# Small products of h (routing logits, selection weights, forget gate) in four groups of 32 array columns

## What is computed

```python
# routing, first block
logit_g = (xt @ w_group + b_group)            # 4 columns
logit_e = (xt @ w_router + b_router)          # 16 columns
# even layer of the second block: weights of the 4 indexer heads that choose 128 keys a row
qa, ka, va, qi, ki, wi, qb, kb, vb = _split(xn @ w_in, EVEN_SPLITS)   # wi: 4 columns
score = jnp.einsum('bqhs,bqh->bqs', rel, wib)
# odd layer: forget gate of 8 heads
log_f = jax.nn.log_sigmoid(fc + forget_b)     # fc: 8 columns of xn @ w_in
f_cum = lax.cumsum(log_f, axis=1)             # added to the logits of the attention
```

## Time and profile before

| | |
|---|---|
| median of 3 runs | 1798.04 us (1797.51 to 1798.15) |
| the profiled execution's own time | 1798.52 us |
| its span (first to last instruction of the trace) | 1796.6 us |
| PE busy | 1772.3 us, 99% of the span |
| PEld, DVE, ACT, POOL busy | 1429.6, 1074.1, 932.5, 606.2 us |
| mean granted clock of PE | 0.996 of full speed |

### The profile page before, as it was taken

How to read it: one execution, slowest core, us unless ns; L and a number is a source line. 1 busy time by engine, 2 the same in 40 slices (tenths; PEclk the granted TensorE clock), 3 DMA queues, 4 the chain that set the end, 5 groups by cost and what they waited for, 6 DMA issues and landing times.

```text
span 1796.6 us, 24203 instructions
## 1 busy us (share of the span) xinstructions
PE 1772.3 (99%) x8498; PEld 1429.6 (80%) x8498; DVE 1074.1 (60%) x1971; ACT 932.5 (52%) x1601; POOL 606.2 (34%) x341
## 2 busy tenths in 40 slices
PE   7999999999999999999999999999999999999997
PEld 5888767888888777787888888887777888888887
DVE  6677747999999599855555554223345655555113
ACT  6667645888887355555444443223555544444221
POOL 2332233111111233233444444443431444444442
PEclk9999999999999999999999999999999999999999
DMA  8322246999997222332223323333431233223332
GB/s 307 136 72 83 81 166 215 365 382 389 382 385 304 68 82 85 92 94 71 94 94 100 100 94 97 97 100 106 139 97 36 94 103 97 94 95 100 98 97 69
DMA packets 71256, 258.78 MB, mean 144 GB/s; under 512 B 13547, under 2 KB 18795, under 8 KB 58744
## 3 DMA queue, kind: packets, MB, share of 16 engines
q1 hardware_dynamic: 66520, 250.19, 40.9%
q0 software_dynamic: 4640, 7.32, 1.1%
HBM read 247.52 MB, written 18.43 MB: 148 GB/s over the span
## 4 chain that ended last, share of the span: by engine, by line
PE 60%; DVE 5%; issue 0%; POOL 0%; DMA 0%; SPq 0%; ACT 0%; DVEq 0%
PE ps L215 18%; PE ps L216 18%; PE ps L217 18%; DVE selb L1369 2%; DVE m L1368 1%; PE ps L569 1%; PE ps L608 1%; PE ps L597 1%; DVE prob L798 1%; DVE prob L813 1%; PE ps L583 0%; PE ps L616 0%; DVE selb L1346 0%; PE ps L631 0%; PE ps L637 0%
## 5 line engine op out<-in xcount | busy, mean ns | idle before, releaser
L282 POOL TENSOR_TENSOR ring_wl<-ring_w,ring_wh 128x1024 fp32r<-128x1024 f32 (+1 forms) x224 | 528.6, 2362 | 904.2 <-ACT ring_wh L274 798.5
L215 PE MATMUL ps<-two_x_high,ring_wh 128*128 128x512 f32 x1064 | 418.8, 394 | 0.7 <-DVE nmax L798 0.6
L216 PE MATMUL ps<-two_x_low,ring_wh 128*128 128x512 f32 x1064 | 414.2, 389 | 0.0
L217 PE MATMUL ps<-two_x_high,ring_wl 128*128 128x512 f32 x1064 | 414.2, 389 | 0.0
L274 ACT CAST ring_wh<-ring_w 128x1024 fp32r<-128x1024 f32 (+1 forms) x228 | 235.8, 1035 | 224.8 <-PE ps L217 222.3
L215 PEld LDWEIGHTS ps<-two_x_high,ring_wh 128*128 128x128 f32 x1064 | 199.7, 188 | 46.9 <-issue 2.2
L216 PEld LDWEIGHTS ps<-two_x_low,ring_wh 128*128 128x128 f32 x1064 | 199.7, 188 | 42.0 <-issue 1.4
L217 PEld LDWEIGHTS ps<-two_x_high,ring_wl 128*128 128x128 f32 x1064 | 199.7, 188 | 41.7
L1125 ACT ACTIVATE acc<-ps,param 128x512 f32<-128x512 f32 x88 | 68.6, 780 | 172.0 <-DVE ps L1145 172.0
L215 PE MATMUL ps<-hid_high,ring_wh 128*128 128x512 f32 (+1 forms) x374 | 141.0, 377 | 0.0
L216 PE MATMUL ps<-hid_low,ring_wh 128*128 128x512 f32 (+1 forms) x374 | 140.8, 377 | 0.0
(11 more groups left out here) (366 smaller groups left out, 3256.0 us busy)
## 6 DMA issues: line engine op xcount, KB each, us to landing
ring_w<-in_w_ff_up SPq DMA_DIRECT2D x88, 512.0 KB, 3.6
one_wg<-in_w_gate SPq DMA_DIRECT2D x32, 1024.0 KB
one_wu<-in_w_up SPq DMA_DIRECT2D x32, 1024.0 KB
one_wd<-in_w_down SPq DMA_DIRECT2D x32, 1024.0 KB, 9.6
ring_w<-in_w_ff_down SPq DMA_DIRECT2D x32, 448.0 KB, 3.3
ring_w<-in_w_da SPq DMA_DIRECT2D x23, 512.0 KB, 3.9
ring_w<-in_w_ff_down SPq DMA_DIRECT2D x16, 512.0 KB, 3.5
ring_w<-in_w_rel SPq DMA_DIRECT2D x12, 512.0 KB, 3.7
```

The costliest lines, as they stand in the source:

```text
L215: mm(out, wh, xh, start=start, stop=False)
L216: mm(out, wh, xl, start=False, stop=False)
L217: return mm(out, wl, xh, start=False, stop=stop)
L282: eng.tensor_tensor(self.low[s][:, 0:k, :], self.slab[s][:, 0:k, :], self.high[s][:, 0:k, :].bitcast(F32), ALU.subtract).then_inc(self.spl ...
```

## The change

All three small projections become full fp32 products of weights and unsplit state. For the gate and the selection, POOL first multiplies the weights by the gain of the norm, so that the state is `h` itself; the rounding by ACT and the low parts are gone. Chunk j goes to the group of 32 array columns with the number j modulo 4, that is to PSUM partitions 32(j mod 4) and on; chunks 0 to 3 begin the four sums, 4 to 7 end them. The four partial sums are added by DVE: for the gate with a copy and three additions, for the other two in a reduction over four elements after the transposes, which are now of all 128 rows.

The order changes too. The logits of chunks 0 to 3 run in one go behind m = 5, 4 and 5 behind m = 7, 6 and 7 behind the transposes of chunk 6. Of the gate's products, four run before the first projection of the odd attention, and four, with the mean, inside it before its chunk 4. At the start of stage "two" ACT rounds two slabs before it computes the root, and DVE, not POOL, makes the rest of the first.

```diff
@@ Select
     def tensor_weigh(self, pe):
-        c, x, buf = self.c, self.norms.x, self.buf
+        c, buf = self.c, self.buf
         pe.wait_ge(self.w_ok, 1)
+        pe.wait_ge(self.norms.added, DC)
         for j in range(DC):
-            mm = c.product(c.ps[0:4, 3, :], (buf["wwh"][:, j, :], buf["wwl"][:, j, :]),
-                           (x[0][:, j, :], x[1][:, j, :]), j == 0, j == DC - 1)
-        mm.then_inc(self.weighed, 1)
+            at = 32 * (j % 4)
+            c.nc.tensor.matmul(c.ps[at:at + 4, 3, :], buf["ww"][:, j, :], c.h[:, j, :], start=(j < 4), stop=(j >= 4))\
+             .then_inc(self.weighed, 1)
...
         for tt in range(TT):
-            mm = nc.tensor.transpose(c.ps[:, 3, 8 * tt:8 * tt + 4], self.buf["wiT"][0:4, P * tt:P * tt + P],
-                                     c.k("ident")[0:4, 0:4])
+            mm = nc.tensor.transpose(c.ps[:, 3, P * tt:P * tt + P], self.buf["wiT"][:, P * tt:P * tt + P], c.k("ident"))
...
-        nc.vector.tensor_copy(wi[:, :, :], c.ps[:, 3, 0:8 * TT].rearrange("p (t e) -> p t e", t=TT)[:, :, 0:4])\
-          .then_inc(self.wi_ok, 1)
+        nc.vector.tensor_reduce(wi[:, :, :], c.bank(3).rearrange("p (t g e) -> p t e g", t=TT, g=4)[:, :, 0:4, :],
+                                AX_X, ALU.add).then_inc(self.wi_ok, 1)
@@ Gate
-    def tensor(self, pe, k):
-        c, buf, x = self.c, self.buf, self.norms.x
+    def tensor(self, pe, k, chunks):
+        c = self.c
         pe.wait_ge(self.w_ok, 1)
-        for j in range(DC):
-            pe.wait_ge(self.norms.xlow, 8 * k + j + 1)
-            mm = c.product(c.ps[0:8, 2, :], (buf["wfh"][:, j, :], buf["wfl"][:, j, :]),
-                           (x[0][:, j, :], x[1][:, j, :]), j == 0, j == DC - 1)
-        mm.then_inc(self.projected, 1)
+        for j in chunks:
+            at = 32 * (j % 4)
+            pe.wait_ge(self.norms.added, 8 * k + j + 1)
+            c.nc.tensor.matmul(c.ps[at:at + 8, 2, :], self.buf["wf"][:, j, :], c.h[:, j, :], start=(j < 4), stop=(j >= 4))\
+             .then_inc(self.projected, 1)
...
-        dve.wait_ge(self.projected, 1)
+        dve.wait_ge(self.projected, DC)
+        nc.vector.tensor_copy(x[:, :], c.ps[0:8, 2, :]).then_inc(self.joined, 1)
+        for group in range(1, 4):
+            dve.wait_ge(self.joined, group)
+            nc.vector.tensor_tensor(x[:, :], c.ps[32 * group:32 * group + 8, 2, :], x[:, :], ALU.add).then_inc(self.joined, 1)
+        dve.wait_ge(self.joined, 4)
         dve.wait_ge(self.norms.inverted, k + 1)
-        nc.vector.tensor_tensor(x[:, :], c.ps[0:8, 2, :], self.norms.rs[0:8, :], ALU.mult).then_inc(self.step, 1)
+        nc.vector.tensor_tensor(x[:, :], x[:, :], self.norms.rs[0:8, :], ALU.mult).then_inc(self.step, 1)
@@ Outward
+        def logits(chunks):
+            for i in chunks:
+                pe.wait_ge(self.whole_ok, i + 1)
+                group = slice(32 * (i % 4), 32 * (i % 4) + 32)
+                nc.tensor.matmul(c.ps[group, 2, :], wr[:, i, :], xw[:, i, :], start=(i < 4), stop=(i >= 4))\
+                  .then_inc(self.logits, 1)
...
-            if m == 3:
-                chunk(0)
-            chunk(m - 2)
-        chunk(6)
-        chunk(7, rows=False)
+            for i in (0, 1) if m == 3 else (m - 2,):
+                pe.wait_ge(self.whole_ok, i + 1)
+                if m == 7:
+                    logits((4, 5))
+                turn(i)
+            if m == 5:
+                logits(range(4))
+        pe.wait_ge(self.whole_ok, 7)
+        turn(6)
+        logits((6, 7))
@@ Route.vector
-        then(tt_(L[:, :, :], c.ps[:, 3, 0:32 * TT].rearrange("p (t e) -> p t e", t=TT)[:, :, 0:20],
-                 buf["rsc"][:, :].unsqueeze(2).broadcast_to([P, TT, 20]), ALU.mult))
+        then(nc.vector.tensor_reduce(L[:, :, :], c.bank(3).rearrange("p (t g e) -> p t e g", t=TT, g=4)[:, :, 0:20, :],
+                                     AX_X, ALU.add))
+        then(tt_(L[:, :, :], L[:, :, :], buf["rsc"][:, :].unsqueeze(2).broadcast_to([P, TT, 20]), ALU.mult))
@@ second_half
-                for i in range(3):
+                for i in (1, 2):
                     ring.rest(pool, at["a0"] + i)
...
+                def rest_of_gate(pe):
+                    gate.tensor(pe, 2, range(4, DC))
+                    norms.mean(pe, 2)
...
-                gate.tensor(pe, 2)
-                norms.mean(pe, 2)
-                att[1].tensor(pe, lambda pe: norms.columns(pe, 2))
+                gate.tensor(pe, 2, range(4))
+                att[1].tensor(pe, lambda pe: norms.columns(pe, 2), inside=rest_of_gate)
...
+                for i in range(2):
+                    ring.round(act, at["a0"] + i)
                 norms.invert(act, 0)
-                for i in range(3):
-                    ring.round(act, at["a0"] + i)
                 act.wait_ge(c.cleared, 1)
-                gate.scalar_weights(act)
+                ring.round(act, at["a0"] + 2)
...
                 dve.wait_ge(c.cleared, 1)
+                ring.rest(dve, at["a0"])
                 select.vector_evacuate(dve)
```

More of the change, by code:

```diff
@@ L556, in gpsimd, with tensor @@
                 ring.rest(pool, self.job(r, i) + 3)
-    def tensor(self, pe, after_q=None, after_k=None, after_v=None, turned_v=None, before_scores=None):
+    def tensor(self, pe, after_q=None, after_k=None, after_v=None, turned_v=None, before_scores=None, inside=None):
         c, nc, ring, buf, x = self.c, self.c.nc, self.ring, self.buf, self.norms.x
@@ L644, in tensor, with ready @@
             if r == 0:
-                project(0, 0, self.x_ready)
+                def ready(pe, j):
+                    if j == 4 and inside:
+                        inside(pe)
+                    pe.wait_ge(self.norms.xlow, 8 * self.k + j + 1)
+                project(0, 0, ready)
                 if after_q:
@@ L1171, in __init__ @@
         self.c, self.ring, self.j0, self.norms, self.buf = c, ring, j0, norms, buf
-        (self.w_in, self.w_high, self.w_ok, self.weighed) = (
-            st.sem(f"sel_{n}") for n in ("w_in", "w_high", "w_ok", "weighed"))
+        self.w_in, self.w_ok, self.weighed = (st.sem(f"sel_{n}") for n in ("w_in", "w_ok", "weighed"))
     def begin(self, st, buf):
@@ L1248, in tensor_free @@
         pe.wait_ge(self.reluded, 12)
[L1250 to L1253, removed]
     def gpsimd(self, pool):
[L1256 to L1259, removed]
+        ww, gain = self.buf["ww"], self.c.p("g_mix2", 0, DC)
+        pool.wait_ge(self.w_in, 16)
+        self.c.nc.gpsimd.tensor_tensor(ww[:, :, :], ww[:, :, :], gain.unsqueeze(2).broadcast_to([P, DC, 4]), ALU.mult)\
+            .then_inc(self.w_ok, 1)
     def scalar_square(self, act):
@@ L1288, in vector_evacuate @@
             nc.vector.tensor_tensor(buf["sraw"][:, i, :], c.bank(i), rs[:, :], ALU.mult).then_inc(self.evac, 1)
-        dve.wait_ge(self.weighed, 1)
-        nc.vector.tensor_tensor(buf["wiT"][0:4, :], c.ps[0:4, 3, :], rs[0:4, :], ALU.mult).then_inc(self.evac, 1)
+        dve.wait_ge(self.weighed, DC)
+        nc.vector.tensor_tensor(buf["wiT"][:, :], c.bank(3), rs[:, :], ALU.mult).then_inc(self.evac, 1)
     def vector_after_q(self, dve):
@@ L1383, in __init__ @@
         self.c, self.norms, self.buf = c, norms, buf
-        (self.w_in, self.w_high, self.w_ok, self.projected, self.biased, self.ast, self.lg, self.step,
+        (self.w_in, self.joined, self.w_ok, self.projected, self.biased, self.ast, self.lg, self.step,
          self.written) = (st.sem(f"gate_{n}") for n in (
-             "w_in", "w_high", "w_ok", "projected", "biased", "ast", "lg", "step", "written"))
+             "w_in", "joined", "w_ok", "projected", "biased", "ast", "lg", "step", "written"))
     def load(self, sp):
@@ L1394, in store @@
         sp.wait_ge(self.written, 16)
[L1396 to L1399, removed]
     def gpsimd(self, pool):
[L1402 to L1405, removed]
-    def tensor(self, pe, k):
-        c, buf, x = self.c, self.buf, self.norms.x
-        pe.wait_ge(self.w_ok, 1)
-        for j in range(DC):
-            pe.wait_ge(self.norms.xlow, 8 * k + j + 1)
-            mm = c.product(c.ps[0:8, 2, :], (buf["wfh"][:, j, :], buf["wfl"][:, j, :]),
-                           (x[0][:, j, :], x[1][:, j, :]), j == 0, j == DC - 1)
-        mm.then_inc(self.projected, 1)
+        wf, gain = self.buf["wf"], self.c.p("g_mix2", DC, DC)
+        pool.wait_ge(self.w_in, 16)
+        self.c.nc.gpsimd.tensor_tensor(wf[:, :, :], wf[:, :, :], gain.unsqueeze(2).broadcast_to([P, DC, 8]), ALU.mult)\
+            .then_inc(self.w_ok, 1)
+    def tensor(self, pe, k, chunks):
+        c = self.c
+        pe.wait_ge(self.w_ok, 1)
+        for j in chunks:
[3 more added lines that the diff above has]
+             .then_inc(self.projected, 1)
     def scalar(self, act):
@@ L1992, in scalar @@
         act.wait_ge(self.logits, 8)
-        nc.scalar.copy(buf["lgT"][0:20, :], c.ps[0:20, 2, :]).then_inc(self.lg_copied, 1)
```

(6 more changed lines are left out.)

10 lines of the change are left out of this document (3 added, 7 removed).

## The result

The changed kernel takes 1788.41 us (median of 6 runs, 1786.64 to 1790.25) against 1797.65 us (6 runs, 1796.97 to 1798.15): ratio 0.9949, 95% interval 0.9937 to 0.9962, 9.2 us less. The forecast was 1789.2, with 1786.5 to 1794.0. The profiled execution took 1788.05 us (span 1786.2).

What follows compares the result with a forecast made beforehand. PE was taken to bound the kernel, busy 1772.3 of 1796.6 us. Routing 4.25, selection 3.05 and gate 1.5 sum to 8.8 us: 1789.7 against the profiled 1798.52, 1789.2 for the median, range 1786.5 to 1794.0.

Steps and rivals of the forecast that it cites:

- The price of a batch: Small projections: four full products in four column groups cost 1.06 us, as one does; two batches in a row 1.9.
- pairs: Small projections: groups overlap only in pairs, a batch costs 1.9 us, gain 4.9, time 1793.1; chance 0.09.
- one after another: Small projections: groups of 32 don't overlap, a batch costs 3.9 us, 5.4 slower, time 1803.4; chance 0.06.
- A: Routing: one batch instead of five separate products ahead of the end of m = 7, tail at nothing; gain 4.25 us.
- The case named beside it: Routing: if the half-clock stretch went away, DVE's chain would be the limit and the gain some 0.3 us more.
- no new wait in routing ahead of the prefix sums: Routing, sign expected in the profile after: PE gets no new wait ahead of the prefix sums.
- my own text on the tail: Routing behind m = 7: chunk 6's turn needs ACT's earlier copy, so the last pair starts no earlier; cost nothing.
- B: Selection weights, start of stage two: two batches replace 24 products, then the first slab binds; gain 3.05 us (2.0 to 3.6).
- C: Forget gate: PE is 3.3 us earlier, but bias and masks bind the first shift; gain 1.5 us (0.7 to 3.3).
- So the chain stays where it was: Forget gate: the multiplication starts at 1228.4 instead of 1228.52, the masks end at about 1249.85 instead of 1249.94.
- The rest: Expert stage between and second layer: they merely shift, with no gain or loss.
- third rival: Small projections: groups of 32 don't overlap; masks end at 1255.2, 5.4 us slower, time 1803.4; chance 0.06.

Runs made afterwards that it cites:

- b_only: The kernel before with only the selection weights' part of the change, including its order of engines at the start of stage two: 1794.54 us.
- four_together: The changed kernel with routing's logits of chunks 4 to 7 in one batch behind m = 7, transposes of chunks 6 and 7 last: 1789.92 us.
- both_warm: The changed kernel with logits 4 to 7 in one batch, all gate products ahead of the projection, and five products without use instead of four: 1785.24 us.
- pool_rest: The changed kernel with the first slab's rest in stage two made by POOL, as before, instead of DVE: 1789.10 us.
- a_only: The kernel before with only the routing's part of the change: 1793.20 us.
- c_only: The kernel before with only the forget gate's part of the change: 1794.37 us.
- gate_whole: The changed kernel with all eight gate products ahead of the projection and the mean of squares ahead of its chunk 2: 1787.21 us.
- neighbours: The changed kernel with chunk j in group j // 2 instead of j modulo 4, so two products in a row share a group: 1791.86 us.
- one_group: The changed kernel with the selection weights' eight full products all in the first group of 32 columns: 1791.83 us.
- four_warm: The changed kernel with logits 4 to 7 in one batch behind m = 7, run once more with no further edit: 1788.63 us.

## Why the prediction was right, and where not

**The price of a batch: right.** 1.04 to 1.06 us, and 1.90 for two. Here the Trainium skill, page "TensorE: Matmul & The Clock Gate", section "Measured speedup vs the span model", gives 3.07 times for four row tiles; an estimate of a batch from it is about 1.3 us. For these four column groups the trace disagrees: 1.04 to 1.06, what one costs. Nor do the rows bear out what the Trainium skill says on the same page, in the note "The full XBUS picture", of the fourth quadrant ("not supported"): the batch of 1.06 us has its fourth product in PSUM partitions 96 and on. Both rivals that rested on the groups (pairs, one after another) are out by the same rows.

**A: 4.39 against 4.25, right in its batches, and behind them by luck.** Up to the end of m = 7 it is 4.28 (265.22 - 235.53 = 29.69 before, 260.58 - 235.18 = 25.40 now) against 4.24. The reduction took 0.49, as the 0.48 worked out; DVE's chain is 0.54 longer (5.16 to 5.70). The case named beside it came: the half clock was absent, and DVE's chain became the limit. Then nothing covers the longer chain: b_only's routing, old and at full clock, has a wait of 0.72 for the matrix, the changed one 1.25, 0.53 more. Against an execution before without the stretch the gain of A is 43.69 - 40.01 = 3.7. So the 4.39 holds only against a profile that had the stretch, and the loss of the stretch (0.7) and the longer chain (0.5) nearly cancel there. The sign "no new wait in routing ahead of the prefix sums" failed twice: 1.14 for ACT's copy ahead of the turn of chunk 6, which my own text on the tail implied, and the 1.25. It is the first that `four_together` and `both_warm` turned into 1.4 us; the second stayed at 1.25 in `four_together`.

**B: right in mechanism, 2.84 against 3.05.** `project(0, 0)` came 2.36 behind the first product (2.4 forecast) after a wait of 0.46 (0.4). `pool_rest` shows that the first slab binds. The loss in layer 0 was 0.36, not 0.1: the four transposes took 0.50 (611.65 to 612.15) where the small ones took 0.31 (619.99 to 620.30), and `project(0, 0)` itself 5.64 instead of 5.54, since its first product behind the wait is slower (605.68 to 605.99); 0.07 is untraced.

**C: the step that was mis-sized.** "So the chain stays where it was": up to the store it did. The multiplication started 7.98 behind the first product (forecast 7.94), the store 13.24 (13.32 before). But the masks started 12.24 behind the store instead of 12.77. I had taken the 12.77 of one profile as fixed, and it is not: with the same old gate, a_only has 12.25 and b_only 11.37. Among the kernels with the new order of the gate c_only has 11.80 and the eight that take over the whole change with it 12.12 to 12.46. The two profiles of the changed kernel have 12.24 and 12.29, the two of `four_together` 12.24 and 12.46. What sets the time of these loads no run shows. And I took 1.5 where my own sum gave 1.7. With the masks 0.6 earlier and `project(1, 1)` 0.5 instead of 0.6 behind the shift that gives the measured 2.34. The new wait for the shift is 0.84, not 1.6. That the bias binds was right: `gate_whole`, which only moves that chain, gained 1.2 by the cut.

**The rest.** 0.55 less in the experts was not forecast; as c_only shows, it needs no change in routing, and its cause is open. The start (0.36) is no effect. The forecast of 1789.2 is 0.8 above the median: 0.4 of it because the kernel before came out at 1797.65 in six runs, not 1798.04, and 0.4 because the medians moved by 9.2, not 8.8. That last agreement is closer than the parts: C gave 0.8 more and layer 0 took 0.26 more than forecast. In the third rival the masks end at about 1255.45 by its own figures (1249.85 and 5.6), not 1255.2; it did not come, so nothing hangs on it.

## What to carry to other kernels

A full product with at most 32 columns of weights cost here as much alone (1.03 us) as four did side by side (1.06). Put independent sums into four groups of columns, add them at the end, and price a batch by its fullest group, in whatever order the program names them. Then read what the next product waits for: here a slab's rest, a bias that goes through DRAM, and a chain of small DVE operations each took over within 0.5 to 1.3 us, and moving work around the last two gave another 2.6 us by the cuts of `both_warm` (3.3 by the medians). Do not take the length of such a chain from one profile: the loads here varied by 1.4 us in three kernels with the same gate. When a wait of PE moves, look at the granted clock of the work behind it; a product without use in the wait may be worth more than the wait.

## What the runs showed of the hardware

- Products in different column groups run at once, and not in program order (`neighbours`): four in two groups took 1.92 us, two turns, where an ordered start would have needed three.
- Four products in four groups cost 1.04 to 1.06 us, one costs 1.03; eight in four groups 1.90, in one group 7.03.
- The clock does not follow the sum of the waits. With waits of 1.14, 0.57, 1.25 and 0.59 us in routing PE kept 2.4 GHz there in all six profiles that have them (the changed kernel twice, `a_only`, `gate_whole`, `pool_rest`, `one_group`). With shorter ones it fell to 1.2 GHz for about 3.4 us around the last of them and the gathers: 0.29, 0.57, 1.26 and 0.59 in `neighbours`; 0.20, 0.20, 0.14, 1.25 and 0.59 in `four_together`, and again when run as `four_warm`, with 1.23 and 0.21 at the end. With the 1.25 cut to 0.39 (`both_warm`, one profile) it stayed up. In the kernel before the stretch came in two of the three profiles of unchanged routing (before, c_only; not b_only), so one profile with or without it proves little.
- The time from the gate's store to POOL's first mask, through DRAM and the bias loads, was 11.2 to 12.8 us over the 14 profiles, and 12.77, 12.25 and 11.37 in three kernels that do not differ in the gate.
